# Spreading the six value products of an attention mixer one per key unit

## The reference

```python
q = (rms_norm(cq_in, g_cq) @ w_q_up).reshape(B, N, MLA_HEADS, MLA_QK)
kv = (rms_norm(ckv_in, g_ckv) @ w_kv_up).reshape(B, N, MLA_HEADS, MLA_NOPE + MLA_V)
k_nope, v = kv[..., :MLA_NOPE], kv[..., MLA_NOPE:]
k_rope = jnp.broadcast_to(kr_in[:, :, None, :], (B, N, MLA_HEADS, MLA_ROPE))
q, k = rms_norm(q, g_q), rms_norm(concatenate([k_nope, k_rope]), g_k)   # then rotary on latent tokens
```

## Time and profile before

| what | value |
|---|---|
| median of 3 runs | 2892.13 us (2889.28 to 2896.05) |
| profiled execution, its own time | 2889.44 us |
| its span, first to last instruction | 2887.6 us |
| mean granted TensorE clock | 0.996 |
| PE busy | 2807.2 us, 97% |
| DVE busy | 1482.7 us, 51% |
| ACT busy | 947.4 us, 33% |
| POOL busy | 263.3 us, 9% |
| DMA | 262.99 MB, mean 91 GB/s |

### The profile page before, as it was taken

One profiled execution on the slowest core, in us unless ns is written; L12 is line 12 of the kernel. 1 busy time (PEld: TensorE's weight loads), 2 busy tenths in 40 slices (PEclk: granted clock), 3 DMA queues, 4 the chain that ended last, 5 costly groups with the idle time before them and its releaser, 6 DMA issues.

```text
span 2887.6 us, 42480 instructions
## 1 busy us (share of the span) xinstructions
PE 2807.2 (97%) x16327; PEld 2646.7 (92%) x16327; DVE 1482.7 (51%) x2293; ACT 947.4 (33%) x1526; POOL 263.3 (9%) x279
## 2 busy tenths in 40 slices
PE   7999999999988899999999999999999998999999
PEld 5999999989977789999999999999998987888887
DVE  6554355455477665533553555245346587633332
ACT  3221122233388642211222322112224388532231
POOL 1000000031234210000000100000003234000000
PEclk9999999999999999999999999999999999999999
DMA  6433243223100224322442234133223201233333
GB/s 224 135 122 99 82 137 122 82 63 78 32 14 12 79 74 134 124 85 81 137 133 58 88 117 134 55 123 117 72 65 87 58 14 46 81 95 107 90 100 90
DMA packets 361092, 262.99 MB, mean 91 GB/s; under 512 B 11086, under 2 KB 339188, under 8 KB 359952
## 3 DMA queue, kind: packets, MB, share of 16 engines
q1 hardware_dynamic: 359440, 256.86, 29.5%
q10 hardware_dynamic: 896, 4.46, 0.4%
q0 software_dynamic: 640, 0.09, 0.0%
HBM read 255.08 MB, written 2.10 MB: 89 GB/s over the span
## 4 chain that ended last, share of the span: by engine, by line
PE 89%; ACT 4%; DVE 3%; issue 2%; POOL 1%; DMA 0%; SPq 0%; POOLq 0%; ACTq 0%; DVEq 0%
PE pair L427 24%; PE pair L428 24%; PE pair L435 24%; PE pair L1311 2%; PE pair L1313 2%; PE pair L1312 2%; PE pair L682 2%; PE pmid L2109 2%; PE pair L683 2%; PE pair L684 2%; ACT prob L2180 1%; ACT pt_hi L2165 1%; DVE pt_lo L2254 1%; PE psum L2134 1%; PE psum L2136 1%
## 5 line engine op out<-in xcount | busy, mean ns | idle before, releaser
L427 PE MATMUL pair<-h_lo,w_hi 128*128 128x384 f32 (+1 forms) x2656 | 906.4, 343 | 0.7 <-ACT sg L1102 0.4
L428 PE MATMUL pair<-h_hi,w_hi 128*128 128x384 f32 (+1 forms) x2656 | 905.4, 343 | 0.0
L427 PEld LDWEIGHTS pair<-h_lo,w_hi 128*128 128x128 f32 x2656 | 498.5, 188 | 22.8 <-issue 0.6
L428 PEld LDWEIGHTS pair<-h_hi,w_hi 128*128 128x128 f32 x2656 | 498.8, 188 | 21.3
L403 DVE TENSOR_TENSOR w_lo<-w_raw,w_hi 128x1024 fp32r<-128x1024 f32 (+1 forms) x262 | 349.0, 1332 | 324.5 <-ACT w_hi L396 321.3
L435 PE MATMUL pair<-h_hi,w_lo 128*128 128x384 f32 (+1 forms) x2656 | 513.8, 343 | 0.0
L435 PEld LDWEIGHTS pair<-h_hi,w_lo 128*128 128x128 f32 x2656 | 463.4, 188 | 20.6
L396 ACT ACTIVATE w_hi<-w_raw 128x1024 fp32r<-128x1024 f32 (+1 forms) x262 | 296.2, 1131 | 539.8 <-PE pair L435 507.4
L427 PE MATMUL pair<-s_lo,w_hi 128*128 128x384 f32 (+1 forms) x1100 | 377.7, 343 | 0.0
L428 PE MATMUL pair<-s_hi,w_hi 128*128 128x384 f32 (+1 forms) x1100 | 377.2, 343 | 0.0
L949 DVE SCALAR_TENSOR_TENSOR pmid<-mod_raw,cs_rows 128x1024 f32<-128x1024 f32 x256 | 315.3, 1232 | 74.8 <-DMA mod_raw<-in_w_mod_rows 58.1
(11 more groups left out here) (310 smaller groups left out, 3603.3 us busy)
## 6 DMA issues: line engine op xcount, KB each, us to landing
mod_raw<-in_w_mod_rows SPq DMA_DIRECT2D x64, 1024.0 KB, 4.9
w_raw<-in_w_ffn_gate SPq DMA_DIRECT2D x88, 512.0 KB, 3.8
w_raw<-in_w_ffn_up SPq DMA_DIRECT2D x88, 512.0 KB, 3.8
w_raw<-in_w_ffn_down SPq DMA_DIRECT2D x64, 704.0 KB, 4.6
w_raw<-in_w_in SPq DMA_DIRECT2D x32, 512.0 KB, 4.0
w_raw<-in_w_out SPq DMA_DIRECT2D x12, 512.0 KB, 4.2
w_raw<-in_w_q_up SPq DMA_DIRECT2D x8, 576.0 KB, 4.1
mod_first<-in_w_mod ACTq DMA_DIRECT2D x4, 1024.0 KB, 9.2
```

The source lines that it names most:

```text
L427: eng.matmul(dst, wh, rl, start=k == 0, stop=False)
L428: eng.matmul(dst, wh, rh, start=False, stop=False)
```

## The change

The table now names one value for each of the steps n - 5 to n: value 0 beside key unit 1, and so on to value 4 beside key unit 5, and value 5 in the step after. All six go through the upper halves of the two accumulators. Value products 2 to 5 wait until the value two before has been drained. The calls that rounded values 4 and 5 behind the split of the first keys are gone on ScalarE and VectorE, and TensorE waits for all six values at the attention's start.

```diff
-        VALUES_AT = {-2: (0,), -1: (1, 2), 0: (3,), 1: (4, 5)}
+        VALUES_AT = {-5: (0,), -4: (1,), -3: (2,), -2: (3,), -1: (4,), 0: (5,)}

         def value_bank(l, t):
-            return pair[t % 2][:, 512:1024] if t < 4 else turn_bank(l, len(UNITS[l]) - 2, t - 4)
+            return pair[t % 2][:, 512:1024]

         def value_product(eng, l, t):

-            if t >= 4:
-                u = len(UNITS[l]) - 2
-                eng.wait_ge(*TURN_EV[l][TURN_AT[l][u] - TURN_AT[l][0] + t - 4])
-            elif t >= 2:
+            if t >= 2:
                 eng.wait_ge(v_free, TOK // P * l + t - 1)
             latent_product(eng, t, value_bank(l, t), NOPE, V_DIM).then_inc(v_done, 1)
...
             attention_split_hi(eng, l, 0, slice(1, 2))
-            for t in VALUES_AT[1]:
-                value_hi(eng, l, t)
             attention_act(eng, l)
...
             eng.wait_ge(ev_act, EV_ACT[l + 1])
-            eng.wait_ge(v_free, TOK // P * l + 4)
+            eng.wait_ge(v_free, TOK // P * (l + 1))
             eng.wait_ge(ident_ready, 1)
             for s in range(n + 4):
-                if s == 2:
-                    eng.wait_ge(v_free, TOK // P * (l + 1))
...
             eng.tensor_tensor(lo, src, hi.bitcast(F32), ALU.subtract).then_inc(a_lo, 1)
-            for t in VALUES_AT[1]:
-                value_lo(eng, l, t)
             for s in range(n + 5):
```

## The result

The changed kernel took 2900.82 us (median of 10 runs, 2898.63 to 2903.34); the kernel before, run beside it, 2891.93 us (10 runs, 2889.06 to 2896.05). The ratio is 1.0029, with a 95% interval from 1.0021 to 1.0037: 8.9 us slower. The forecast was 2897.2 us in a range of 2890.5 to 2902, so the sign and the range held, and the time was 3.6 us over the forecast.

The account below looks back on a forecast made before the run. TensorE makes 89% of the whole chain, but ScalarE and VectorE were taken to bound the touched key units. 2.88 us of order plus 2.2 of clock gave +5.1 on 2892.13: 2897.2 us, range 2890.5 to 2902.

Parts of the forecast that it names:

- The order: Mixer's last key units to attention entrance: the new sequence of values alone adds 1.44 us a layer, 2.88 in both.
- The four spacings: Distances between starts of VectorE's sums of squares for key units 1 to 5: 3.33, 3.62, 4.16, 3.62 us.
- the split of keys: ScalarE's split of the first keys at the attention's entrance, 7.24 us after the last sum of squares, before 7.81.
- rival C: At the key units, values fill ScalarE's idle time of about 1.0 us a step: -1.1 us, 2891.0 us; chance 0.10.
- TensorE's queue: At the key units, TensorE needs 3.51 us for a step with a value and is over 2 us ahead of squares.
- the removed waits: Value products' former waits in the mixer's last steps: their removal costs nothing; without TensorE's margin, 0.2 us more a step.
- The pause and the fall of the clock: Ahead of the first score product TensorE idles 5.4 us, so the attention opens at the 1.2 GHz level.
- Rival A: At both attention entrances the clock holds through the pauses, only the order counts: +2.9 us, 2895.0 us; chance 0.20.
- The price of the clock: Slower matmuls at the attention's opening cost 1.1 us a layer, 2.2 in all, between ends of 0.9 and 2.7.
- the 0.95 and the 1.3: Clock costs in us at the attention's opening for low stretches of 3.4 and 6.8 us, largely covered by ScalarE and VectorE.
- the upper end: At the attention's opening, the low level lasts through four score blocks and the first six transposes: +2.7 us.
- Rival B: In both layers the low level outlasts the attention's first blocks and TensorE paces them: +8.3 us, 2900.4 us; chance 0.18.

Follow-up runs that it names:

- the last three experiments: Late values with entrance waits filled, 2892.03 us; the same plus matmuls at later places, 2889.07; kernel before with all extra matmuls, 2888.53; kernel before beside them, 2891.43.

## Why the prediction was right or wrong, point by point

**The order: right, to 0.05 us.** The four spacings were put at 3.33, 3.62, 4.16 and 3.62 us and came at 3.33, 3.61, 4.15 and 3.62; the split of keys at 7.24 us behind the last sum, as said. The order was priced at 1.44 us a layer; with the clock held up by extra matmuls it is 1.44 and 1.47. So "all six values are on the path instead of four" is what happened, and rival C, that they fall into holes, is out: ScalarE's 1.0 us of idle time stands ahead of the root, where nothing behind it in the order can use it.

**TensorE's queue: right in effect, wrong in its margin.** The prediction had TensorE over 2 us ahead of the squares. From the end of the unit's last matmul, as the profile models it, to ScalarE's square it was 0.16 us for k2, 0.44 for k3, 1.18 for k4 and 1.00 for k5 in layer 0 of the changed kernel (and by as little as 0.04 for k2 in the kernel before). No square waited for it, so the removed waits cost nothing, but there was little to spare ahead of k2.

**The pause and the fall of the clock: right.** A pause of 5.4 us was forecast, 5.32 came, and the clock was down in both layers. The Trainium skill's rule ("TensorE: Matmul & The Clock Gate", Part 1), that only activity lifts the throttled clock, agrees with the kernel with ten matmuls fewer a layer (clock 0.55 and 0.69 behind the first score product, 6.7 us slower), and with the one with 24 more a layer (1.00, 5.6 us faster than the change). What the trace adds is that the changed kernel did 10.8 us of nearly unbroken work there before the clock was back. Rival A is out.

**The price of the clock: wrong, too small.** This is the term of the sum that was mis-sized: "for both the score blocks are largely covered by ScalarE's and VectorE's work on the first two chunks, which gives 0.95 and 1.3. I take 1.1 a layer". It measured 3.03 and 3.19 us a layer (35.46 - 32.43 and 35.33 - 32.14). The prediction shows no working for the 0.95 and the 1.3. Two things were mis-sized. First, the stretch: I took 3.4 to 6.8 us from the earlier trace rows, and it went on for 10.8 us behind the first score product (clock 0.51 over the whole window of 11), through four score blocks and twelve transposes. Why it lasted longer than those is not shown; TensorE was as busy at the low level here (10.79 of 11 us) as there. Second, even the upper end, 2.7, was short of what was measured, since it stopped at the second chunk's transposes. Up to those it was good: they start 9.68 us after the first score product (823.79 - 814.11), 2.62 later than before. The first block alone cost 0.97 us, close to the 0.9 of the working; the other 2.1 came over the next three exponentials (+0.24, +0.77, +1.07), as TensorE became the engine that the others wait for.

**Rival B named this**: the low level outlasting the first blocks, in both layers, +8.3 us. Measured +8.9. It was given 0.18, and its point of decision, 7 us past the first score product, was passed. The two readings of the price were 1.1 and 2.7 for the same mechanism; the low value was chosen by the length of stretches seen elsewhere, past the opening behind waits of 1.7 to 2.3 us, and this pause was of 5.3. The length of the pause alone doesn't set the stretch either: behind the 2.58 us that twelve extra matmuls left, it was 10.2 us. That the measured time lies in the range is owed to this rival, to which the range was drawn; the forecast's own sum had 2.2 us for the clock where 6.2 came.

**The 11.6 us between the two profiled spans** are 2.5 more than the entrances explain. They lie where low stretches fall differently in the two executions: the opening gives -0.5 us and chunks 45 to 47 of layer 0 -1.35, the stretch between the two attentions +1.9 (TensorE waits 2.7 us for the pooling mixer ahead of 2189 us, and the clock fell there in the profiled execution of the change and not in that of the kernel before), and the third neighbourhood head of layer 1 +2.3. The profiled execution of the kernel before is also 2.5 us below its median, so the medians are 8.9 apart and not 11.6.

## What to carry to other kernels

Before moving matmuls out of a wait, look at what TensorE does in that wait: products that seem to cost nothing may be what keeps its clock up for the stage that follows, and in the profiled execution with twelve extra matmuls a pause of 2.6 us ahead of the attention was followed by 10 us at half speed. Then count the operations on the chain before and after, by place and not by the engines' idle time: spreading six values evenly put two more on the chain, since an engine that works in a fixed order can't take up later work while it waits for an earlier step. And the extra matmuls that paid here covered the whole pause without delaying what came behind it; half of them gave 0.2 us a layer, and those put late ran at the low level in front of the path in one of two layers.

## What the runs showed of the hardware that was not expected

The low level of the clock lasted far longer at the attention's entrance (13.65 us in both layers of the changed kernel, of which 10.8 and 10.9 us lie behind the first score product with TensorE busy 98% of the time) than in the opening of the kernel (6.8 us) or at single late waits (3.4 or 6.8 us). With 12 matmuls at the start of the pause it was 10.2 us, in both layers. What sets the length isn't shown.

The same pause can give either result. Ahead of the twelve late matmuls TensorE waited 3.53 us in one layer and 3.54 in the other, and the clock fell in the first alone. At the wait for the pooling mixer it fell after 2.74 us in the changed kernel and held after 2.69 in the one with 24 extra matmuls a layer. The spread of the runs of the kernel before, 2888 to 2895 us beside the last three experiments, goes with the mean granted clock: of these 27 runs the nine shortest (2888.1 to 2890.1 us) had 0.996 or 0.997, the seven longest (2894.0 to 2895.3 us) 0.993 to 0.995.
